# Loading the state-space parameters in long pieces, turning C earlier, and spreading the extra sums of two MLP blocks

## The reference, cut to what matters

```
z = RMSNorm(x) ;  u, q, k, v, g, gate_a, gate_b = split(z @ W_in)
branch A (state space), 32 groups x 16 channels, one 64-dim complex state per group:
  step = exp(log_step); a = exp((lam_re + i lam_im) * step); k = (a - 1) / lam
  h[t] = a * h[t-1] + (k * B) u[t];  y = Re(C h) + d_skip * u
  y = gelu(y);  y = y * sigmoid(y @ W_glu + b_glu)
branch B: retention with 4 heads on q, k, v, gated by g
h = x + (sigmoid(gate_a) * (y_A @ P_A) + sigmoid(gate_b) * (y_B @ P_B)) @ W_out
h = h + relu(RMSNorm(h) @ W_up)^2 @ W_down          (d_ff = 4096)
out = RMSNorm(h)
```

## Time and profile before

| | us |
|---|---|
| median of 3 runs | 1580.9 |
| the runs | 1576.4, 1580.9, 1580.96 |
| the profiled execution | 1576.09 |
| its span, first to last instruction | 1574.2 |
| TensorE busy | 1516.3 (96%) |
| DVE busy | 946.2 (60%) |
| GpSimd busy | 426.8 (27%) |
| ScalarE busy | 300.9 (19%) |

### The profile page before, as it was taken

How to read it: one execution, slowest core, us unless ns; L and a number is a source line. 1 busy time by engine, 2 the same in 40 slices (tenths; PEclk the granted TensorE clock), 3 DMA queues, 4 the chain that set the end, 5 groups by cost and what they waited for, 6 DMA issues and landing times.

```text
span 1574.2 us, 21201 instructions
## 1 busy us (share of the span) xinstructions
PE 1516.3 (96%) x7440; PEld 1269.3 (81%) x7440; DVE 946.2 (60%) x1918; ACT 300.9 (19%) x577; POOL 426.8 (27%) x359
## 2 busy tenths in 40 slices
PE   5898999999999999999999998999999999999996
PEld 4786888778888888878888877888888888888885
DVE  6788756553564646475624788655555555555557
ACT  4121111220222222132101322111111111111114
POOL 1210010421000010103433004344444444444444
PEclk9999999999999999999999999999999999999998
DMA  5423434354201010212552010111111111111113
GB/s 161 129 94 89 118 99 131 109 166 163 74 28 53 17 50 13 67 41 97 185 180 68 0 41 14 54 54 53 53 53 53 48 46 53 53 53 53 43 49 122
DMA packets 105748, 119.18 MB, mean 76 GB/s; under 512 B 23520, under 2 KB 73824, under 8 KB 105696
## 3 DMA queue, kind: packets, MB, share of 16 engines
q1 hardware_dynamic: 74704, 78.23, 16.2%
q10 hardware_dynamic: 30992, 40.26, 8.1%
HBM read 96.57 MB, written 20.97 MB: 75 GB/s over the span
## 4 chain that ended last, share of the span: by engine, by line
PE 83%; DVE 10%; SPq 2%; ACT 1%; ACTq 1%; DMA 1%; issue 1%; POOL 0%; DVEq 0%
PE acc L631 20%; PE acc L633 20%; PE acc L632 20%; PE aux L632 5%; PE aux L633 5%; PE aux L631 5%; SPq L396 1%; PE aux L875 1%; PE aux L869 1%; PE aux L878 1%; PE aux L762 1%; DMA stage<-in_w_in 1%; ACTq L1143 1%; DVE tb L1776 1%; PE aux L768 1%
## 5 line engine op out<-in xcount | busy, mean ns | idle before, releaser
L2086 DVE TENSOR_TENSOR h_res<-h_res,acc 128x512 f32<-128x512 f32 x240 | 160.5, 686 | 101.2 <-PE acc L633 99.9
L631 PE MATMUL acc<-dw_hi,hid_hi 128*128 128x512 f32 x512 | 200.8, 392 | 6.9 <-DVE h_res L2086 6.2
L632 PE MATMUL acc<-dw_lo,hid_hi 128*128 128x512 f32 x512 | 200.5, 392 | 0.0
L633 PE MATMUL acc<-dw_hi,hid_lo 128*128 128x512 f32 x512 | 200.4, 391 | 0.0
L631 PE MATMUL acc<-w_hi,z_hi 128*128 128x256 f32 (+1 forms) x512 | 189.2, 370 | 0.0
L631 PE MATMUL acc<-z_hi,w_hi 128*128 128x512 f32 x448 | 179.6, 401 | 9.7 <-DVE z_lo L1464 5.0
L509 POOL CAST w_hi<-stage 128x1024 fp32r<-128x1024 f32 x44 | 48.4, 1117 | 495.2 <-PE acc L633 322.1
L633 PE MATMUL acc<-z_hi,w_lo 128*128 128x512 f32 x448 | 176.9, 395 | 0.0
L632 PE MATMUL acc<-z_lo,w_hi 128*128 128x512 f32 x448 | 176.8, 395 | 0.0
L633 PE MATMUL acc<-w_hi,z_lo 128*128 128x256 f32 (+1 forms) x512 | 173.2, 338 | 0.0
L632 PE MATMUL acc<-w_lo,z_hi 128*128 128x256 f32 (+1 forms) x512 | 173.1, 338 | 0.0
(11 more groups left out here) (315 smaller groups left out, 2920.8 us busy)
## 6 DMA issues: line engine op xcount, KB each, us to landing
stage<-in_w_up SPq DMA_DIRECT2D x32, 512.0 KB, 4.0
stage<-in_w_down SPq DMA_DIRECT2D x32, 512.0 KB, 3.4
stage<-in_w_in SPq DMA_DIRECT2D x28, 512.0 KB, 4.6
gate_dram<-gate_t ACTq DMA_DIRECT2D x32, 256.0 KB, 2.0
x_in<-in_x SPq DMA_DIRECT2D x8, 512.0 KB, 8.1
stage<-in_w_in SPq DMA_DIRECT2D x32, 128.0 KB, 2.7
stage<-in_w_in SPq DMA_DIRECT2D x16, 256.0 KB, 3.3
gb_t<-gate_dram ACTq DMA_DIRECT2D x16, 256.0 KB, 3.2
```

What stands on the lines that cost most here:

```text
L631: nc.tensor.matmul(out, s_hi, m_hi_, start=first, stop=False)
L632: nc.tensor.matmul(out, s_hi, m_lo_, start=False, stop=False)
L633: return nc.tensor.matmul(out, s_lo, m_hi_, start=False, stop=last)
L2086: V.tensor_tensor(h_res[:, c, hs], h_res[:, c, hs], acc[:, p % 4, :], ALU.add)\
```

## The change

Three things. First, lam_re, lam_im, d_skip and b_glu are loaded as rows of 128 values (16, 16, 4 and 4 rows) into one tile `prm`, log_step as 16 rows of 2 values, which DVE spreads over 64 columns each. These transfers stand early in SyncE's queue: log_step behind the first chunk of x, the four others behind `ident`. TensorE turns `prm` with two transposes behind chunk 0, ACT copies the result out in three copies. B and C come straight after x, ahead of weight pieces 2 and 3. Second, TensorE turns C behind the first feature tile of U's second half, ACT copies it out behind the sixth U tile, and DVE's low parts of the first two gate pieces move behind the coefficients. Third, in the plain blocks the sums and low parts that stood before the first addition move between the additions.

```diff
+            prm = sb("prm", [P, P], F32, r)
+            ls_raw = sb("ls_raw", [P, 16], F32, r)
...
@@ SyncE
             sp.dma_start(x_in[:, 0, :], x_rows[:, 0, :]).then_inc(x_ready[0], 16)
+            sp.dma_start(ls_raw[STATE:STATE + PAIRS, 0:2], t["log_step"].rearrange("a (q e) -> (a q) e", e=2),
+                         allow_slow_non_contiguous=True).then_inc(ls_in, 16)
             sp.dma_start(x_in[:, 1, :], x_rows[:, 1, :]).then_inc(x_ready[1], 16)
...
             sp.dma_start(ident[:], t["ident"]).then_inc(ident_in, 16)
+            for i, name in enumerate(("lam_re", "lam_im")):
+                sp.dma_start(prm[i * PAIRS:(i + 1) * PAIRS, :], t[name][0].rearrange("(q e) p -> q (e p)", e=2))\
+                  .then_inc(lam_in, 16)
+            for i, name in enumerate(("d_skip", "b_glu")):
+                r0 = 2 * PAIRS + i * MT
+                sp.dma_start(prm[r0:r0 + MT, :], t[name].rearrange("a (m p) -> (a m) p", p=P)).then_inc(lam_in, 16)
...
             for gp, rows in enumerate(halves):
-                sp.dma_start(coef[rows, 2, :], bass.AP(tensor=ls.tensor, offset=gp, ap=[[0, STATE], [2, PAIRS]]),
-                             allow_slow_non_contiguous=True).then_inc(lam_in, 16)
-                for i, name in enumerate(("lam_re", "lam_im")):
-                    sp.dma_start(coef[rows, i, :], t[name][0, gp::2, :].rearrange("g p -> p g"),
-                                 allow_slow_non_contiguous=True).then_inc(lam_in, 16)
-            for i in range(2, 4):
-                load(i, w_in[:, 2 * i:2 * i + 2, 0:HALF])
-            for gp, rows in enumerate(halves):
+                for ri, name in enumerate(("c_re", "c_im")):
+                    sp.dma_start(c_raw[:, ri, :, gp * STATE:(gp + 1) * STATE],
+                                 t[name][0].rearrange("(m g) c p -> (g c) m p", m=MT)).then_inc(par_in, 16)
                 for ri, name in enumerate(("b_re", "b_im")):
...
+            for i in range(2, 4):
+                load(i, w_in[:, 2 * i:2 * i + 2, 0:HALF])
@@ TensorE
-            for c in range(4):
+            turn_x(0)
+            pe.wait_ge(lam_in, 16 * 4)
+            pe.wait_ge(ls_wide, 1)
+            nc.tensor.transpose(acc[:, 3, 0:40], prm[0:40, :], ident[0:40, 0:40])
+            nc.tensor.transpose(acc[:, 3, 40:40 + PAIRS], prm[STATE:STATE + PAIRS, :],
+                                ident[STATE:STATE + PAIRS, STATE:STATE + PAIRS]).then_inc(prm_turned, 1)
+            for c in range(1, 4):
                 turn_x(c)
...
+            pe.wait_ge(prm_ready, 1)
             quad(OUT_U, GR_U % 2, KT, z_hi, z_lo, 0, LD_U + 1, hooks={1: (4,), 2: (5,), 4: (6,), 5: (7,)})
...
                 features(OUT_U + MT + m, GR_U % 2, KT, m * P, z_hi, z_lo, 1)
+                if m == 0:
+                    turn_c()
@@ ScalarE
             hi_z(0)
+            act.wait_ge(prm_turned, 1)
+            nc.scalar.activation(coef[:, 0:2, :], acc[:, 3, 0:2 * PAIRS].rearrange("p (i q) -> p i q", i=2), ACT.Copy)
+            nc.scalar.activation(skip_glu[:], acc[:, 3, 2 * PAIRS:40].rearrange("p (i m) -> p i m", i=2), ACT.Copy)
+            nc.scalar.activation(coef[:, 2, :], acc[:, 3, 40:40 + PAIRS], ACT.Copy).then_inc(prm_ready, 1)
             hi_z(1)
...
+                if n == 5:
+                    take_ct()
@@ DVE
+            dve.wait_ge(ls_in, 16)
+            V.tensor_copy(prm[STATE:STATE + PAIRS, :].rearrange("p (e s) -> p e s", e=2),
+                          ls_raw[STATE:STATE + PAIRS, 0:2].unsqueeze(2).broadcast_to([PAIRS, 2, STATE])).then_inc(ls_wide, 1)
             rstd_x(0, 1)
...
-            dve.wait_ge(lam_in, 16 * 6)
+            dve.wait_ge(prm_ready, 1)
...
-            gate_lo(0, 0)
-            gate_lo(0, 1)
...
+            gate_lo(0, 0)
+            gate_lo(0, 1)
             powers(pwr, pwi, 1, T)
@@ DVE, plain_block
-                    if f == 0 and n == 3:
-                        form_s2(0)
...
-                    if f == 1 and n == 3:
-                        for u in range(2):
-                            lo_s(1 + u, s2_hi, s2_lo, s2_sum, u)
...
-                    if f == 0 and (j, p) == (0, 7):
-                        form_s2(1)
+                    if f == 0 and j == 0 and p in (5, 7):
+                        form_s2(p // 2 - 2)
...
                     if f == 1 and j == 0 and p in (1, 3):
-                        lo_s(3 + p // 2, s3_hi, s3_lo, s3_sum, p // 2)
+                        lo_s(1 + p // 2, s2_hi, s2_lo, s2_sum, p // 2)
                     if f == 1 and j == 0 and p in (5, 7):
-                        lo_s1(p // 2 - 2)
-                    if f == 1 and j == 1 and p in (2, 5):
-                        lo_s(7 + p // 4, s4_hi, s4_lo, s4_sum, p // 4)
+                        lo_s(1 + p // 2, s3_hi, s3_lo, s3_sum, p // 2 - 2)
+                    if f == 1 and j == 1 and p in (0, 2):
+                        lo_s1(p // 2)
+                    if f == 1 and j == 1 and p in (4, 6):
+                        lo_s(5 + p // 2, s4_hi, s4_lo, s4_sum, p // 2 - 2)
```

More of the change, by code:

```diff
@@ L180, in build @@
         spin = sb("spin", [P, 2, PAIRS], F32, ph)
-        dskip = sb("dskip", [P, MT], F32, ph)
-        bglu = sb("bglu", [P, MT], F32, ph)
+        skip_glu = sb("skip_glu", [P, 2, MT], F32, ph)
+        dskip, bglu = skip_glu[:, 0, :], skip_glu[:, 1, :]
         with ExitStack() as r:
@@ L197, in build @@
             x_junk = sb("x_junk", [P, D], BF16, r)
-            sb("x_pad", [P, 1136], F32, r)
+            prm = sb("prm", [P, P], F32, r)
+            ls_raw = sb("ls_raw", [P, 16], F32, r)
+            sb("x_pad", [P, 992], F32, r)
             coef = sb("coef", [P, 56, PAIRS], F32, r)
@@ L279, in build @@
         lam_in = sem("lam_in")
+        ls_in = sem("ls_in")
+        ls_wide = sem("ls_wide")
+        prm_turned = sem("prm_turned")
+        prm_ready = sem("prm_ready")
         par_in = sem("par_in")
@@ L681, in turn_x, with turn_c @@
                     mm.then_inc(z_turned, 1)
-            pe.wait_ge(ident_in, 16)
-            for c in range(4):
+            def turn_c():
+                pe.wait_ge(par_in, 16 * 8)
+                for ri in range(2):
+                    for m in range(MT):
+                        mm = nc.tensor.transpose(aux[:, ri, m * P:(m + 1) * P], c_raw[:, ri, m, :], ident[:])
+                mm.then_inc(ct_turned, 1)
+            pe.wait_ge(ident_in, 16)
+            turn_x(0)
[5 more added lines that the diff above has]
+            for c in range(1, 4):
                 turn_x(c)
             pe.wait_ge(lo_done, SP_Z + 8)
+            pe.wait_ge(prm_ready, 1)
             quad(OUT_U, GR_U % 2, KT, z_hi, z_lo, 0, LD_U + 1, hooks={1: (4,), 2: (5,), 4: (6,), 5: (7,)})
@@ L693, in _ @@
                 features(OUT_U + MT + m, GR_U % 2, KT, m * P, z_hi, z_lo, 1)
-            pe.wait_ge(par_in, 16 * 10)
-            pe.wait_ge(lo_done, SP_Z + 2 * NCH)
-            for ri in range(2):
-                for m in range(MT):
-                    mm = nc.tensor.transpose(aux[:, ri, m * P:(m + 1) * P], c_raw[:, ri, m, :], ident[:])
-            mm.then_inc(ct_turned, 1)
+                if m == 0:
+                    turn_c()
             def batch(b, steps):
@@ L1082, in _, with take_ct @@
                 hi_z(c)
+            def take_ct():
+                act.wait_ge(ct_turned, 1)
+                for ri, dst in enumerate((ctr, cti)):
+                    for gp in range(2):
+                        rows = slice(gp * STATE, (gp + 1) * STATE)
+                        src = aux[rows, ri, :].rearrange("p (m q e c) -> p m q e c", q=QP, e=2, c=CH)[:, :, :, gp, :]
+                        ins = nc.scalar.activation(dst[rows, :, :].rearrange("p (m q) c -> p m q c", m=MT), src, ACT.Copy)
+                        ins.then_inc(ct_ready, 1) if ri == 1 and gp == 1 else None
             for n in range(8):
@@ L1093, in _ @@
                     act.dma_start(u_dram[m], u_all[:, m, :, :]).then_inc(u_out, 16)
-            act.wait_ge(ct_turned, 1)
-            for ri, dst in enumerate((ctr, cti)):
-                for gp in range(2):
-                    rows = slice(gp * STATE, (gp + 1) * STATE)
-                    src = aux[rows, ri, :].rearrange("p (m q e c) -> p m q e c", q=QP, e=2, c=CH)[:, :, :, gp, :]
-                    ins = nc.scalar.activation(dst[rows, :, :].rearrange("p (m q) c -> p m q c", m=MT), src, ACT.Copy)
-                    ins.then_inc(ct_ready, 1) if ri == 1 and gp == 1 else None
+                if n == 5:
+                    take_ct()
             act.wait_ge(u_out, 16 * MT)
@@ L1675, in wide @@
                 return a.unsqueeze(2).broadcast_to([P, PAIRS, CH])
-            dve.wait_ge(par_in, 16 * 10)
+            dve.wait_ge(par_in, 16 * 8)
             br, bi = b_raw[:, 0, :, :], b_raw[:, 1, :, :]
```

6 lines of the change are left out of this document (removed).

## The result

The changed kernel takes 1560.0 us (median of 4 runs, 1559.2 to 1561.1), the kernel before 1578.7 (4 runs, 1575.0 to 1581.0). The ratio of the runs is 0.988, 95% interval 0.986 to 0.991: about 18 us faster. The forecast was 1559. The profiled execution of the changed kernel takes 1559.25 us, its span is 1557.4. That is 16.8 us under the profiled execution of before, where the sum had 19.5. The total is close, but three of its terms are not, and they cancel in part.

A forecast was written before the change was run, and what follows sets the result against it. TensorE was taken as the bound (busy 96% of the span). Gains 7.5 + 8.7 + 0.6 + 2.7 = 19.5 us gave 1556.6 from the profiled 1576.1 and 1561.4 from the median; it said 1559, own range 1553 to 1564, 8 in 10 1552 to 1569.

The forecast's parts named there:

- the start: Loads before U: five added issues of about 0.45 us each delay x chunk 2 but cost 0, bounds 0 and 2.3 us.
- U, from the first product: Projection U: earlier weight pieces remove TensorE's 4.8 us stop for the split and its clock loss, gain 7.5 us.
- scan of batch 0 with its clock: State-space batch 0: earlier parameters and C remove TensorE's wait for DVE's scan, gain 7.0 us plus 1.74 of clock.
- batches 1 to 3 up to the MLP product of the table above: State space up to block 0's third hidden tile: loop unchanged, waits of 0.57 and 2.75 us stay, gain 0.
- MLP block 0: First plain block: the 1.96 us stop goes, two stops of 0.7 us come; gain 0.6 us, bounds -1 to 2.
- MLP block 1 with the clock: Second plain block: 3.8 us gained if the clock holds behind a new 2.1 us wait, 1.5 if not; taken 2.7.
- rival 4: At the start: chunk 1's turn waits for the parameter transfers, 5.6 us slower in all, 1586 us; chance 0.03.
- rival 2: In U: weight pieces 2 and 3 land no earlier, the stop stays, 7.5 us lost, 1566.5 us; chance 0.06.
- I take 0: In U: GpSimd's passes hold DVE's short operations at no net cost, out of 0 to 6.8 us held.
- Rival 1: In U: DVE is late, from GpSimd beside it or x landing later; 3 us less gain, 1562 us; chance 0.12.
- rival 5: Scan of batch 0: C or coefficients over 3.5 us late; all of the 8.7 us lost gives 1568; chance 0.07.
- Rival 3: Plain MLP blocks: no gain, DVE bounds both and the new wait drops the clock; 3.3 us less, 1562.5; chance 0.10.

The follow-up runs named there:

- e1: The changed kernel with the log_step transfer moved behind ident and DVE's copy of it behind norm_x(0); 1559.9 us.
- e6: The changed kernel with the last four splits of plain MLP block 1 placed one to two additions earlier; 1555.5 us.
- e3: The changed kernel with GpSimd's cast and split of weight piece 2 waiting until DVE has normalised all eight x chunks; 1556.3 us.
- e8: The changed kernel with the edits of e3 and e6 together; 1554.2 us, ratio to before 0.9847.
- e9: The changed kernel unaltered, in a second profiled execution; 1560.1 us, ratio to before 0.9883.
- e5: The kernel before with only the new order of the extra sums in the plain MLP blocks; 1570.9 us beside 1575.3, ratio 0.9976.
- e4: The changed kernel with the turn of C and ACT's four copies of it back behind the whole of U; 1568.8 us, ratio to before 0.995.
- e10: The kernel before with weight pieces 2 and 3 of U issued ahead of the six transfers of 4-byte pieces; 1582.9 us beside 1573.8.
- e2: The changed kernel with log_step and the four other parameter transfers behind x chunk 3, their turn and copies later too; 1557.6 us.
- e7: The changed kernel with the edits of e1, e3 and e6 together; 1552.9 us, ratio to before 0.9843.

## Why the prediction was right, and where it was wrong

The terms, as leads over the kernel before in the profiled executions:

| step | forecast | measured |
|---|---|---|
| the start | 0 | -1.55 |
| U, from the first product | 7.5 | 4.5 |
| scan of batch 0 with its clock | 8.7 | 9.0 |
| batches 1 to 3 up to the MLP product of the table above | 0 | 2.0 |
| MLP block 0 | 0.6 | 1.0 |
| MLP block 1 with the clock | 2.7 | 2.1 |
| behind it | 0 | -0.2 |
| sum | 19.5 | 16.8 |

**The start.** The step took 0 with bounds of 0 and 2.3 us, because x chunk 2's issue lay behind 1.6 MB. Chunk 2 was never the limit; the norm row was, and it is issued behind the log_step transfer. It landed 7.3 us after issue instead of 5.9 (the view of DMA issues), and e1 shows that log_step's place does it. What was mis-sized is the cover: I priced the issues (0.45 us each) and not what a small transfer does to those behind it. The term cost its length: e6 starts 0.87 us earlier than the changed kernel on the same code and keeps 0.79 of it up to the MLP product. By it one sign of being wrong that the prediction gave did show: turn 1 came at 14.27, not by 13. That sign was meant for rival 4, whose cause did not come; the parameters' transposes start at 12.80, right behind chunk 0, with no wait.

**U.** The stop for the split went and the weights were in time (piece 2 was cast from 27.58 on); that step is right, and rival 2 did not come. The step that failed is "I take 0" for the hold of DVE's short operations beside GpSimd, out of 0 to 6.8 us. The value taken from the MLP's passes was the wrong neighbour: there a pass of 1.13 us took 0.8 us more, here an operation of 0.16 us took until GpSimd's instruction ended. Four rstd operations took 1.02, 2.22, 0.94 and 2.25 us instead of 0.16, 5.8 us more; in e3 the normalisation starts 5.7 us earlier (29.27 for 34.97). And the place was another: I looked for the first late consumer among the splits of z, at the seventh turn, while the normalisation, ahead of them on DVE, fed the fifth. The rstd chain, over at 27.65 before, was taken to be over when piece 2 landed (29). Here the chain was 1.55 us later and the cast started at 27.58.

What the hold cost depends on the clock. With the slow first k steps of the changed kernel it cost 1.9 us, as e3 shows (8.31 for 10.23); with the fast ones, 3.0 (7.18 in e8 for 10.15 in e9). So of the 3.05 us to before, 1.1 would have stayed in this execution without the hold, and none in one with the clock of e8. Rival 1 had the mechanism; that its 3 us fit is luck as to the place.

The rule of the Trainium skill that the prediction weighed (SBUF — State Buffer, section "SBUF: two separate sides") is that whoever starts first has the shared port pair for its whole instruction. The rows agree with it: 2.22 us beside GpSimd's 2.36, and 5.7 of the 6.8 us. The page lets the same lock be taken by operations in a two-port mode, and the one-input TENSOR_SCALAR rows of e3 (2.26, 2.37 us) were held too; whether they run in such a mode no row tells.

The slow first k steps are not the change's: e5, with before's code there, takes 8.32 us for them, before 7.34, e9 7.35.

**The scan.** Right in what it gained: DVE's wait for the parameters gone and that for C down from 6.73 to 1.52 us, no stop, the small matmuls in 1.95 us. The memset came at 71.2 and not at 66, since U's first half was late and C's turn with it; 1.4 us of the forecast 3.5 to spare were left. So rival 5 did not come either. e4 shows that it needs the early C: with C late the wait is 6.93 us again.

**Batches 1 to 3.** "Its waits of 0.57 and 2.75 us stay": the first did (0.56), the second became 1.53 with the clock kept. e5 and e10, with before's code in this stage, have 1.53 too, so the 2.6 us are not owed to the change but to the order in which DVE and GpSimd met in one execution of before. Without them the change is worth 14 us between these two executions, where the sum had 19.5. That the whole came so near the forecast is in this part luck. The runs say 18 (14 to 22); the profiled execution of before is at the fast end of its runs, which spread over 7 us (1573.6 to 1581.0, all of them taken together).

**The MLP.** Rival 3 did not come, though the clock fell as it said. Block 0: stops of 0.47 and 0.32 us where 0.7 twice was said. Block 1: the gain of 3.8 us to the first window product came exactly, and the clock fell behind the wait, as half of the forecast had it. The other half is what the same code did in e2 and e3.

## What to carry to other kernels

A short operation on DVE beside GpSimd's long passes on SBUF can take as long as what is left of the pass, not a share more: in this chain of twelve five did. Before a transfer is moved earlier, see what GpSimd's work on it will then stand beside, and let it wait until DVE's short chain is through. Follow each late or early input to what is queued behind its wait on the same engine, not to its last consumer. When a lead at the start does not reach the end, look for the stretch in which it goes; here it was the clock behind a longer stop. And ahead of long TensorE stretches, spend an effort on stops of about 2 us: they may cost their own length again in clock.

## What the runs showed of the hardware that was not expected

- The clock behind a stop of about 2 us is not settled by the stop. After 1.78 to 1.83 us ahead of the window blocks it fell in five executions (changed, e1, e4, e5, e9) and stayed up in two (e2, e3), at 587.8 to 588.5 against 586.2 and 586.3 us to the end. In before it had stayed up after 1.96 us. After 0.41 to 0.45 us (e6, e7, e8) it stayed up each time. Before the fifth turn in U it fell after 2.24 and 2.80 us (e1, e9; 1.55 us lost each) and not after 1.82 to 1.99 (changed, e4, e6, e10).
- The hold works both ways and the order decides. In batch 3 GpSimd's subtraction took 2.38 us in before and 3.25 in e5, where DVE's pass got in first. DVE's two passes behind the scan took 5.2 us in both; its scan took 3.43 us in before, with GpSimd's cast beside its last 1.4 us, and 2.63 in e5. Half a microsecond of phase made 1.2 us on TensorE, and the clock on top.
- With one transfer of 128 bytes in pieces of 8 issued second, the norm row (512 KB, issued two places behind it) was first used at 8.50 to 9.58 us (six executions), without it at 7.87 to 8.11 (six). Of that 0.46 us is its own later issue (2.12 for 1.66). By what mechanism the rest comes is open.
